# Second projection of a two-layer encoder: rounded head sums, their place in the order, and what follows from them

## The reference

```python
h = rms_norm(x, g_pre)
proj = jnp.einsum('btd,de->bte', h, w_in)
q, k, v, gate = jnp.split(proj, SPLIT_C, axis=-1)
q = rms_norm(q.reshape(B, T, C_HEADS, C_HEAD_DIM), q_norm)
k = rms_norm(k.reshape(B, T, C_KV_HEADS, C_HEAD_DIM), k_norm)
q = jnp.concatenate([rope(q[..., :half], rows), rope(q[..., half:], cols)], axis=-1)
k = jnp.concatenate([rope(k[..., :half], rows), rope(k[..., half:], cols)], axis=-1)
```

## Time and profile before

| | us |
|---|---|
| median of 3 runs | 2071.51 |
| lowest, highest | 2070.16, 2072.22 |
| profiled execution | 2070.7 |
| span of its instructions | 2068.9 |
| TensorE busy in the span | 2023.8 |
| VectorE busy | 1224.0 |
| ScalarE busy | 1127.2 |
| GpSimd busy | 947.8 |

### The profile page before, as it was taken

How to read it: one execution, slowest core, us unless ns; L and a number is a source line. 1 busy time by engine, 2 the same in 40 slices (tenths; PEclk the granted TensorE clock), 3 DMA queues, 4 the chain that set the end, 5 groups by cost and what they waited for, 6 DMA issues and landing times.

```text
span 2068.9 us, 25552 instructions
## 1 busy us (share of the span) xinstructions
PE 2023.8 (98%) x9480; PEld 1629.7 (79%) x9480; DVE 1224.0 (59%) x1935; ACT 1127.2 (54%) x1440; POOL 947.8 (46%) x487
## 2 busy tenths in 40 slices
PE   8999998999999999999999999999999999999998
PEld 6878886888888877777887667888777777777888
DVE  6432135325776667663559878624477778776454
ACT  6142234435566666665446444343577778888431
POOL 1222224435555555656102556523566766677501
PEclk9999999999999999999999999999999999999999
DMA  5133468627665753734335232263233342332534
GB/s 197 56 125 128 153 241 324 169 68 156 129 120 111 169 122 85 163 77 158 120 117 185 92 108 107 102 185 102 71 77 82 72 118 71 80 87 89 169 102 168
DMA packets 172143, 261.38 MB, mean 126 GB/s; under 512 B 78754, under 2 KB 89634, under 8 KB 172020
## 3 DMA queue, kind: packets, MB, share of 16 engines
q1 hardware_dynamic: 172020, 259.76, 44.2%
HBM read 161.78 MB, written 97.92 MB: 126 GB/s over the span
## 4 chain that ended last, share of the span: by engine, by line
PE 90%; ACT 3%; DVE 2%; DMA 2%; POOL 1%; issue 1%; SPq 0%; DVEq 0%; ACTq 0%; POOLq 0%
PE SA L1926 13%; PE OP L1972 11%; PE SM L1852 5%; PE SA L533 5%; PE OP L1979 5%; PE OP L533 5%; PE SM L2025 4%; PE SA L2025 4%; PE OP L1078 4%; PE SA L1078 4%; PE OS L533 3%; PE OS L1972 3%; PE OS L1078 2%; PE OS L2025 2%; PE SM L1848 2%; PE OS L1979 1%
## 5 line engine op out<-in xcount | busy, mean ns | idle before, releaser
L2446 POOL TENSOR_TENSOR c_PL<-c_PF,c_PH 128x1024 fp32r<-128x1024 f32 x128 | 307.8, 2408 | 137.5 <-ACT c_PH L2148 79.7
L2446 POOL TENSOR_TENSOR ab_PL<-ab_PF,ab_PH 128x1024 fp32r<-128x1024 f32 (+3 forms) x128 | 264.6, 2067 | 192.4 <-ACT ab_PH L2148 135.9
L2145 ACT ACTIVATE ab_PF<-SA 128x1024 f32<-128x1024 f32 (+3 forms) x160 | 143.7, 898 | 158.3 <-PE SA L1887 85.0
L2145 ACT ACTIVATE c_PF<-SA 128x1024 f32<-128x1024 f32 x160 | 164.0, 1025 | 85.3 <-PE SA L1926 84.3
L2233 DVE TENSOR_REDUCE c_MH<-SM 128x1 f32<-128x512 f32 x256 | 170.9, 684 | 66.5 <-PE SM L1852 66.4
L431 POOL TENSOR_TENSOR e_wl<-e_raw,e_wh 128x1024 fp32r<-128x1024 f32 (+1 forms) x31 | 73.5, 2370 | 191.3 <-ACT e_wh L600 191.3
L2148 ACT ACTIVATE c_PH<-c_PF 128x1024 fp32r<-128x1024 f32 x128 | 135.8, 1061 | 4.1
L1926 PE MATMUL SA<-c_Q,c_KA 128*128 128x512 f32 x320 | 127.8, 399 | 3.3 <-ACT c_PF L2145 3.3
L1926 PE MATMUL SA<-c_Q,c_KB 72*128 72x512 f32 x320 | 127.1, 397 | 0.0
L1852 PE MATMUL SM<-c_KA,c_Q 128*128 128x512 f32 x320 | 125.1, 392 | 0.0
L1010 POOL TENSOR_TENSOR n_wl<-n_raw,n_wh 128x1024 fp32r<-128x1024 f32 (+1 forms) x24 | 53.4, 2225 | 151.5 <-ACT n_wh L1175 151.5
(11 more groups left out here) (538 smaller groups left out, 5950.9 us busy)
## 6 DMA issues: line engine op xcount, KB each, us to landing
c_Q<-qC_hi SPq DMA_DIRECT2D x32, 384.0 KB, 4.9
e_raw<-in_w_tiles SPq DMA_DIRECT2D x20, 512.0 KB, 3.9
n_raw<-in_w_tiles SPq DMA_DIRECT2D x20, 512.0 KB, 3.8
e_XF<-in_xT SPq DMA_DIRECT2D x12, 512.0 KB, 10.6
silu_gate<-e_ta SPq DMA_DIRECT2D x24, 256.0 KB, 2.1
ab_Q<-qA_hi SPq DMA_DIRECT2D x16, 384.0 KB, 5.5
ab_G<-silu_gate SPq DMA_DIRECT2D x24, 256.0 KB, 3.8
ab_res<-in_xT SPq DMA_DIRECT2D x24, 256.0 KB, 2.9
```

The costliest lines, as they stand in the source:

```text
L2145: nc.scalar.activation(used(PF[p], h, s), used(SA, h, s), ACT.Exp).then_inc(e_done, 1)
L2446: nc.gpsimd.tensor_tensor(used(PL[p], h, s), used(PF[p], h, s), used(PH[p], h, s).bitcast(F32), ALU.subtract).then_inc(p_lo[0], 1)
```

## The change

- The squares of a head are split like everything else. ScalarE squares twice, into f32 (`tsq`) and rounded (`tsh`); GpSimd subtracts (`tsl`, new function `low_square`); TensorE adds the high and the low squares with two f32r matmuls by a rounded copy of the constant (`selr`, which ScalarE makes once).
- The head sum of unit n - 2 stands behind the products of unit n, for every n from 6 (before: from unit 8, one to three units behind). The last two stand inside the first pass over the value tiles.
- Ln and Exp are done in place in the `sums` bank (before: into `tsd` in SBUF), three units behind instead of one. The scaled head goes to PSUM (`scaled`: banks 4 and 5 in turn, but for the last three units) instead of back into `ta`. So units 4 to 33 take turns on four banks, n % 4, instead of six.
- On VectorE `finish` is taken apart. At unit n, ahead of the eviction of n, stand now: `low` of n - 4, `scale` of n - 3, and `turn` of n - 1 (the sum of the rotated halves).
- The third sum of squares goes to bank 5, `root` of it moves from ScalarE's unit 5 to 6.
- On GpSimd the low weights stand behind the rotation and the low square; on ScalarE the high weights stand behind the squares. Stores are issued four units behind, and three of them ahead of the loads at unit 34.

The diff, cut to its core:

```diff
+    def sums_after(n):
+        return (n - 2,) if n - 2 in qk and n < v0 else ()
...
-    tsd = [at(f"tsd{i}", [P, CH], F32, REST + 16384 + 2048 * i) for i in range(2)]
+    tsl = [at(f"tsl{i}", [P, CH], F32R, SPLIT_LO + 16384 + 2048 * i) for i in range(2)]
+    tsh = [at(f"tsh{i}", [P, CH], F32R, REST + 16384 + 2048 * i) for i in range(2)]
+    selr = at("headsel_r", [P, P], F32R, SPLIT_LO + 20480)
...
     def bank_of(n):
+        if 4 <= n < v0:
+            return n % 4
         return (n + 2) % 6 if n < gate0 else late_bank(n, gate0, N, (4, 3, 2, 1, 0))
+    SCALED = len(qk) - 3
+    def scaled(i):
+        return acc[4 + i % 2] if i < SCALED else ta[place_of(i)][:]
+    def third_sum(i):
+        return sums[i] if i < 2 else acc[5]
...
         for n in range(N):
+            if n == v0:
+                for m in range(v0 - 4, v0 - 1):
+                    store(m)
             for w in begins[n]:
                 if 1 < w < len(W) - 2:
                     load(sp, w + 2)
-            if n - 2 in qk:
-                store(n - 2)
+            if n - 4 in qk and n < v0:
+                store(n - 4)
+            if n == v0:
+                store(v0 - 1)
...
+        def low_square(n):
+            i = qk.index(n)
+            pool.wait_ge(q_hi, i + 1)
+            nc.gpsimd.tensor_tensor(tsl[i % 2][:], tsq[i % 2][:], tsh[i % 2][:].bitcast(F32), ALU.subtract
+                                    ).then_inc(q_lo, 1)
...
             if n == 6:
                 low_weights(pool, 4)
+            if n in qk:
+                rotate(n)
+                low_square(n)
             for w in splits[n]:
                 if w > 4:
                     low_weights(pool, w)
-            if n in qk:
-                rotate(n)
...
-            pe.wait_ge(q_sq, i + 1)
-            wait_count(pe, q_log, i - 1)
-            nc.tensor.matmul(sums[i % 2], sel[:], tsq[i % 2][:], start=True, stop=True).then_inc(q_sum, 1)
+            pe.wait_ge(q_hi, i + 1)
+            wait_count(pe, r_norm, i - 1)
+            nc.tensor.matmul(sums[i % 2], selr[:], tsh[i % 2][:], start=True, stop=False)
+            pe.wait_ge(q_lo, i + 1)
+            nc.tensor.matmul(sums[i % 2], selr[:], tsl[i % 2][:], start=False, stop=True).then_inc(q_sum, 1)
...
                 for i in range(TT):
                     if q == 0 and i % 2 == 0:
-                        pe.wait_ge(acc_read, n0 + i // 2 - 5)
+                        wait_count(pe, acc_read, last_user(bank_of(n0 + i // 2), n0) + 1)
+                    if q == 0 and i in (3, 9):
+                        head_sums(v0 - 2 + i // 9)
+                    if q == 0 and i == 8:
+                        pe.wait_ge(lo_done, SCALED)
...
             if n < v0:
-                for m in {8: (4, 5), CATCH: (n - 3, n - 2), v0 - 1: (n - 2, n - 1)}.get(
-                        n, (n - 3 + n // CATCH,) if n > 8 else ()):
+                for m in sums_after(n):
                     head_sums(m)
...
             nc.scalar.activation(tsq[i % 2][:], ta[place_of(i)][:], ACT.Square).then_inc(q_sq, 1)
+            nc.scalar.activation(tsh[i % 2][:], ta[place_of(i)][:], ACT.Square).then_inc(q_hi, 1)
...
+            if n == 6:
                 root(act, 2)
...
+            for m in range(n - 3, n) if n == v0 else (n - 3,):
+                if m in qk and n <= v0:
+                    head_scale(m)
+                    high(m)
...
             if n in qk:
                 square(n)
-            if n - 1 in qk:
-                high(n - 1)
+            if n < v0:
+                for w in splits[n]:
+                    if w > 4:
+                        high_weights(act, w)
...
-        def finish(n):
+        def turn(n):
             i = qk.index(n)
             s = place_of(i)
             dve.wait_ge(r_cos, i + 1)
             dve.wait_ge(r_sin, i + 1)
-            dve.wait_ge(q_sq, i + 1)
+            dve.wait_ge(q_hi, i + 1)
             nc.vector.tensor_tensor(ta[s][:], ta[s][:], tb[s][:], ALU.add).then_inc(r_sum, 1)
+        def scale(n):
+            i = qk.index(n)
             dve.wait_ge(r_sum, i + 1)
             dve.wait_ge(q_rstd, i + 1)
-            nc.vector.tensor_tensor(ta[s][:], ta[s][:], tsd[i % 2][:], ALU.mult).then_inc(r_norm, 1)
+            wait_count(dve, lo_done, i - 1)
...
+            nc.vector.tensor_tensor(scaled(i), ta[place_of(i)][:], sums[i % 2], ALU.mult).then_inc(r_norm, 1)
...
+            if n in qk:
+                if n - 4 in qk:
+                    low(n - 4)
+                if n - 3 in qk:
+                    scale(n - 3)
+                if n - 1 in qk:
+                    turn(n - 1)
             if n >= gate0:
                 between(n - gate0, 0)
             if n > 1:
                 evict(dve, n)
...
-            if n - 1 in qk and n != v0:
-                finish(n - 1)
-            if n - 2 in qk and n < v0:
-                low(n - 2)
```

More of the change, by code:

```diff
@@ L252, in entry @@
     mm_done, acc_read = ar.sem("p_mm_done"), ar.sem("p_acc_read")
-    l_sq, l_add, l_norm, l_hi, l_lo = (ar.sem(f"p_l_{n}") for n in ("sq", "add", "norm", "hi", "lo"))
+    l_sq, l_add, l_norm = (ar.sem(f"p_l_{n}") for n in ("sq", "add", "norm"))
+    l_hi, l_lo = ar.sem("p_part_hi"), ar.sem("p_part_lo")
     hi_done, lo_done = ar.sem("p_hi"), ar.sem("p_lo")
@@ L824, in inner @@
         ("values", u, 2, 512) for u in range(4)] + [("x", t, 8, D) for t in (12, 13, 14, 15, 16, 10, 17, 11)]
-    EARLY, CATCH = 4, 20
+    EARLY = 4
     U = [(tiles[t], t, c) for c in ORDER[0:2] for t in range(2)]
@@ L870, in inner @@
     q_sq, q_sum, q_log, q_rstd = (ar.sem(f"p_q_{n}") for n in ("sq", "sum", "log", "rstd"))
+    q_hi, q_lo = ar.sem("p_part_hi"), ar.sem("p_part_lo")
     r_swap, r_cos, r_sin, r_sum, r_norm = (ar.sem(f"p_r_{n}") for n in ("swap", "cos", "sin", "sum", "norm"))
@@ L1094, in square_sum @@
         def square_sum(i, x):
-            wait_count(pe, deviation, i - 1)
-            nc.tensor.matmul(sums[i % 2], ones[:], x, start=True, stop=True).then_inc(total, 1)
+            nc.tensor.matmul(third_sum(i), ones[:], x, start=True, stop=True).then_inc(total, 1)
         def x_square_sum(c):
@@ L1106, in head_sums @@
             if i == 0:
-                pe.wait_ge(tab_in, 96)
-            if i < 3:
-                pe.wait_ge(deviation, 3 - i % 2)
-            pe.wait_ge(q_sq, i + 1)
-            wait_count(pe, q_log, i - 1)
-            nc.tensor.matmul(sums[i % 2], sel[:], tsq[i % 2][:], start=True, stop=True).then_inc(q_sum, 1)
+                pe.wait_ge(sel_set, 1)
+            if i < 2:
+                pe.wait_ge(deviation, i + 1)
+            pe.wait_ge(q_hi, i + 1)
[3 more added lines that the diff above has]
+            nc.tensor.matmul(sums[i % 2], selr[:], tsl[i % 2][:], start=False, stop=True).then_inc(q_sum, 1)
         def values(n0):
@@ L1159, in tensor @@
                 pe.wait_ge(before.y_sq, NC * KT - 2)
+            if n == 7:
+                pe.wait_ge(acc_read, 4)
             if n in (0, 2, 7):
@@ L1192, in root @@
         out = rstd[:, cols(ORDER[i])]
-        nc.scalar.activation(out, sums[i % 2], ACT.Ln, bias=epst[:], scale=1.0 / D).then_inc(deviation, 1)
+        nc.scalar.activation(out, third_sum(i), ACT.Ln, bias=epst[:], scale=1.0 / D).then_inc(deviation, 1)
         act.wait_ge(deviation, i + 1)
@@ L1228, in head_scale @@
             act.wait_ge(q_sum, i + 1)
-            wait_count(act, r_norm, i - 1)
-            nc.scalar.activation(tsd[i % 2][:], sums[i % 2], ACT.Ln, bias=epst[:], scale=1.0 / HD
-                                 ).then_inc(q_log, 1)
+            nc.scalar.activation(sums[i % 2], sums[i % 2], ACT.Ln, bias=epst[:], scale=1.0 / HD).then_inc(q_log, 1)
             act.wait_ge(q_log, i + 1)
-            nc.scalar.activation(tsd[i % 2][:], tsd[i % 2][:], ACT.Exp, scale=-0.5).then_inc(q_rstd, 1)
+            nc.scalar.activation(sums[i % 2], sums[i % 2], ACT.Exp, scale=-0.5).then_inc(q_rstd, 1)
         def high(n):
@@ L1240, in high @@
                 act.wait_ge(r_norm, qk.index(n) + 1)
-                nc.scalar.activation(out, ta[place_of(qk.index(n))][:], ACT.Copy).then_inc(hi_done, 1)
+                nc.scalar.activation(out, scaled(qk.index(n)), ACT.Copy).then_inc(hi_done, 1)
                 return
@@ L1254, in scalar @@
                 high_weights(act, 4)
+            if n == 6:
                 root(act, 2)
-            for w in splits[n]:
-                if w > 4:
+            if n >= v0:
+                for w in splits[n]:
+                    if w < V0 + 2 or n > v0:
+                        high_weights(act, w)
+            if n == EARLY:
+                act.wait_ge(tab_in, 96)
+                nc.scalar.activation(selr[:], sel[:], ACT.Copy).then_inc(sel_set, 1)
+            for m in range(n - 3, n) if n == v0 else (n - 3,):
+                if m in qk and n <= v0:
+                    head_scale(m)
+                    high(m)
+            if n == v0:
+                for w in splits[v0][1:]:
                     high_weights(act, w)
```

(25 more changed lines are left out.)

13 lines of the change are left out of this document (7 added, 6 removed).

## The result

The changed kernel takes 2080.22 us (median of 4, 2079.41 to 2081.43), the kernel before beside it 2071.28: a ratio of 1.0045 with a 95% interval of 1.0032 to 1.0057, slower by some 9 us where 6 were forecast. Its profiled execution took 2079.41 with a span of 2077.4, 8.5 more than before.

What follows compares the result with a forecast made beforehand. VectorE's ring of 6.27 us per unit was to replace TensorE as the bound; start wait, ring units and the value wait put the gate 6.0 us later: 2070.7 + 6.0 = 2076.7 (median 2077.5), range 2067 to 2090.

Steps and rivals of the forecast that it cites:

- The ring: Evict, squares, rotation, turn, next evict close a loop once per unit: 6.27 us, more than TensorE's 5.90.
- Head sums: On TensorE two rounded matmuls at 0.45 us replace one of 0.87: unit 6.32 to 5.90, hidden by the ring.
- Low weights and scaling: On GpSimd low weights make the next cos late, 2.1 us in all; second table scaling adds at most 0.5.
- Scale and low at nothing: On VectorE both lie in the wait between shuffle and turn, one input in PSUM: no added time.
- rival 2: GpSimd holds scale or low on VectorE too, despite the PSUM operand: 12 us, 2089.5; chance 0.08.
- The start: TensorE waits behind unit 6 for unit 4's low square: unit 7 13.2 us late, evict(6) at 1157.1.
- The values: Third value tile waits some 4.5 us for unit 33's accumulator: first gate unit at 1365.4 against 1359.42.
- the clock behind a long wait: TensorE's granted clock stays low behind the waits at unit 6 and the third value tile: 1.7 us each.
- the doubled charge: Upper bound for lost clock behind TensorE's long wait: twice the 1.7 us charged.
- Rival 1: Turn on VectorE runs unheld beside the low square: ring 5.2, TensorE's 5.90 the bound, 2058.4 us; chance 0.15.
- Rival 3: Rounded head-sum pair on TensorE costs 0.87 as before: at most 1.4 us; counted within the held turn's 0.77.

Runs made afterwards that it cites:

- e1: Changed kernel with turn of n-1 put behind the eviction of n on VectorE: 2059.45 us, ratio 0.9946 to the kernel before.
- e7: Changed kernel with e1's edit, head sums of units 4, 5 behind unit 8, of 6, 7 behind 9, then two behind: 2053.66 us, ratio 0.9915.
- e8: Changed kernel with idle matmuls, results unread, filling three TensorE waits: 2074.47 us, ratio 1.0015 to the kernel before.
- e3: Changed kernel with GpSimd's low square issued as two halves of 256 columns: 2066.75 us, ratio 0.9979 to the kernel before.
- e2: Changed kernel with only the head sums put back to their places in the kernel before: 2080.57 us, ratio 1.0048.
- e6: Changed kernel with head sums of units 4, 5 and 6 behind unit 8, later ones two units behind: 2074.93 us, ratio 1.0022.
- e5: Changed kernel with the edits of e1 and e2 together: 2058.05 us, ratio 0.9936 to the kernel before.
- e9: As e7, but head sum of unit 6 behind unit 9 and those of 7, 8 behind unit 10: 2053.03 us, ratio 0.9913.

## Why the prediction held, step by step

**The ring, 6.27: right, 6.30,** and term by term within 0.05. e1 shows that it is the bound and not a companion of it: with the turn elsewhere the same instructions run at TensorE's 5.89.

**Head sums 0.45 and hidden: right.** 0.227 apart, the unit of 5.89 shows only where the turn is out of the way (e1, e7).

**Low weights and scaling, 2.6: 2.2.** The 27 units took 172.27 us (171.9 forecast), 27 x 6.30 = 170.1 of it the ring.

**Scale and low at nothing: right,** 0.70 and 0.67 in 54 instructions; rival 2 had no ground.

**The start: the mechanism right, the size short.** Unit 7 started at 1147.76 (1147.4 forecast). But it then took 7.85 us, to 1155.61, and not the 7.15 charged, and the eviction of unit 6 came at 1158.11, not 1157.1; 0.29 of it had been there at unit 4.

**The values: right in place, short in the clock in this execution.** The wait was 3.99 (4.5); from the eviction of 33 to the gate 37.50 instead of 36.4.

**The mis-sized term** is the clock behind a long wait. It was taken as 1.7 us a place from the 2.68 us wait of the earlier trace rows; e8 measures 2.6 and 2.65 against the profiled execution. The two differences make 1.85 of the 2.5 us by which the gate came later than forecast (1367.88 against 1365.4). At the start the other traces bear this out: behind the wait of 2.68 before, seven products stand 0.43 apart instead of 0.227, and in unit 7 of the changed kernel, of e1 and of e3 eleven do (the unit took 7.85, 7.77 and 7.67, and 5.46 in e8). At the values they don't: e2 and e6 have the same wait of 3.99 there and then took 36.26 and 36.38 to the gate, 1.4 and 1.5 more than e8's 34.85, less than the charged 1.7. So the price behind one and the same wait differs from execution to execution, and how much of the 2.65 belongs to the kernel stays open; e8's median gain of 5.75 says only that the two places together cost well over the 3.4 charged. The prediction had the doubled charge as an end of its range, and both places went towards that end together.

**Rival 1** (the turn not held, 2058.4) fell with the first held turn; e1 reaches nearly its number, 2059.45, by taking the turn out from beside the low square. Its point of decision, a turn under 1.3 us, was not enough: e3's 1.16 puts the ring at 5.74, under TensorE's 5.90, but with the low weights of every third unit the mean stays at 6.00, and no eviction there waits for TensorE. **Rival 3** is excluded by the 0.227.

What the prediction didn't see is what e2 and e5 found: low weights behind the rotations and sums two units behind depend on each other, so the change couldn't have been had without the start wait by putting the sums back where they were.

## What to carry to other kernels

When an instruction is moved ahead of another on an in-order engine, follow who waits for what until the path comes back to that engine: if it closes, its length is the new unit time, whatever the busiest engine saved. Price a VectorE instruction with two SBUF inputs by what GpSimd does at that moment, and put it where GpSimd pauses, or make the GpSimd instruction beside it shorter. Move the consumer of a late operand on TensorE back only as far as buffers and weights behind it allow, and count the clock behind the wait, not the wait alone.

## What the runs showed that was not expected

- Halving an instruction of GpSimd made the changed kernel faster by 13.5 us although GpSimd became slower (1.89 us for 1.29).
- A turn that was held also slows GpSimd: low weights of 128 x 1024 take 2.80 to 2.87 us in the changed kernel, where the turn gets in ahead of them, and 2.35 to 2.43 in the kernel before, e1 and e3, where it doesn't.
- A wait of 2.90 us (e9) was followed by more lost clock, 2.6 us, than a row of waits of 2.85, 1.35 and 1.62 (1.8, in e7): taking the smaller waits away gained 2.3 us in the stage and no clock.
- The same wait of 3.99 us was followed by 1.4, 1.5 and 2.65 us of lost clock in three executions (e2, e6 and the changed kernel, each against e8).
- Matmuls whose results nobody reads made the changed kernel 5.75 us faster in the median; in the profile the granted clock behind the filled waits read 1.00, and the two places took 5.2 us less.
